# Stick-breaking attention: background passes dealt out otherwise, the logarithm ahead of a copy, VectorE's small work in other places

## The reference, cut to what matters

```
log_keep = where(mask, log_sigmoid(-z), 0)
suffix = reverse_cumsum(log_keep) - log_keep
w = where(mask, exp(log_sigmoid(z) + suffix), 0)
out = w @ v
```

## Time and profile before

| | |
|---|---|
| runs | 2551.66 us median of 3 (2549.52 to 2555.72) |
| profiled execution | 2550.52 us |
| its span, first to last instruction | 2548.7 us |
| mean granted TensorE clock | 0.992 of full speed |
| PE busy | 2456.3 us (96%), 12198 matmuls |
| DVE busy | 1605.5 us (63%) |
| ACT busy | 1094.4 us (43%) |
| POOL busy | 212.7 us (8%) |
| attention stage, first background pass to the product after the stage | 642.4 to 1003.99 us |

### The profile page before, as it was taken

The page is one execution under the profiler, slowest core; times in us unless marked ns, Lnnn a source line. Parts: engine busy times, 40 slices in busy tenths (PEclk is TensorE's granted clock), DMA queues, the critical chain, the costliest instruction groups (busy, mean ns, idle before and its releaser), DMA issues.

```text
span 2548.7 us, 30875 instructions
## 1 busy us (share of the span) xinstructions
PE 2456.3 (96%) x12198; PEld 2011.7 (79%) x12198; DVE 1605.5 (63%) x2065; ACT 1094.4 (43%) x1782; POOL 212.7 (8%) x351
## 2 busy tenths in 40 slices
PE   6999999999999999999999999999999999999997
PEld 5888888888777777878888776887777888888886
DVE  7887565555666666375652555157747767778779
ACT  6665322333666666123421336234435445443333
POOL 0011111111000000100010003000001212200000
PEclk9999999999999999999999999999999999999999
DMA  4223333334122121624123410110232454674432
GB/s 143 91 100 108 100 106 113 105 108 140 63 79 69 52 80 66 251 92 174 40 96 126 132 34 18 50 34 17 76 131 94 156 159 143 212 285 149 149 132 100
DMA packets 139146, 278.50 MB, mean 109 GB/s; under 512 B 16765, under 2 KB 91178, under 8 KB 132218
## 3 DMA queue, kind: packets, MB, share of 16 engines
q1 hardware_dynamic: 109354, 176.52, 20.9%
q0 software_dynamic: 29648, 100.00, 11.1%
HBM read 196.79 MB, written 79.69 MB: 108 GB/s over the span
## 4 chain that ended last, share of the span: by engine, by line
PE 81%; DVE 8%; ACT 5%; DVEq 2%; DMA 2%; issue 2%; ACTq 1%; SPq 0%; POOL 0%
PE ps L2640 32%; PE ps L597 12%; PE ps L3271 8%; PE ps L2891 6%; PE ps L2739 4%; PE ps L2695 2%; PE ps L591 2%; PE ps L2713 2%; PE ps L3165 1%; DVE c L1979 1%; PE ps L2955 1%; PE ps L2876 1%; PE ps L2724 1%; PE ps L3150 1%; PE ps L2804 1%
## 5 line engine op out<-in xcount | busy, mean ns | idle before, releaser
L1894 DVE TENSOR_TENSOR proj_out<-ps,proj_out 128x512 f32<-128x512 f32 x292 | 194.8, 685 | 209.8 <-PE ps L2640 197.1
L2640 PE MATMUL ps<-a_hi,pw_hi 128*128 128x512 f32 x528 | 207.2, 392 | 0.8 <-ACT proj_out L1239 0.8
L2640 PE MATMUL ps<-a_lo,pw_hi 128*128 128x512 f32 x528 | 205.5, 389 | 0.0
L2640 PE MATMUL ps<-t_hi,pw_hi 128*128 128x512 f32 x464 | 182.0, 392 | 0.0
L2640 PE MATMUL ps<-t_lo,pw_hi 128*128 128x512 f32 x464 | 180.7, 389 | 0.0
L2640 PE MATMUL ps<-a_hi,pw_lo 128*128 128x512 f32 x352 | 137.2, 390 | 0.0
L577 DVE TENSOR_TENSOR w_lo<-w_raw,w_hi 128x2048 fp32r<-128x2048 f32 x28 | 64.1, 2288 | 115.8 <-ACT w_hi L573 110.4
L573 ACT ACTIVATE w_hi<-w_raw 128x2048 fp32r<-128x2048 f32 x28 | 53.6, 1913 | 161.9 <-DMA w_raw<-in_w_out 66.0
L1979 DVE TENSOR_TENSOR_SCAN c<-l,r 128x128 f32<-128x128 f32 (+7 forms) x64 | 86.7, 1355 | 54.5 <-ACT l L1363 54.4
L2640 PEld LDWEIGHTS ps<-a_hi,pw_hi 128*128 128x128 f32 x528 | 99.1, 188 | 21.1 <-issue 1.2
L2640 PEld LDWEIGHTS ps<-a_lo,pw_hi 128*128 128x128 f32 x528 | 99.2, 188 | 20.2
(11 more groups left out here) (498 smaller groups left out, 6621.8 us busy)
## 6 DMA issues: line engine op xcount, KB each, us to landing
pw_raw<-in_w_in SPq DMA_DIRECT2D x30, 1024.0 KB, 5.3
hidden_raw<-hidden_forms SPq DMA_DIRECT2D x28, 1024.0 KB, 4.8
projections<-proj_out POOLq DMA_DIRECT2D x88, 256.0 KB, 3.0
w_raw<-in_w_in SPq DMA_DIRECT2D x18, 1024.0 KB, 5.1
pw_raw<-in_w_ff SPq DMA_DIRECT2D x16, 1024.0 KB, 6.3
w_quarter<-in_w_ff SPq DMA_DIRECT2D x16, 1024.0 KB, 7.2
hidden_forms<-proj_out POOLq DMA_DIRECT2D x56, 256.0 KB, 3.2
hidden_forms<-nb POOLq DMA_DIRECT2D x56, 256.0 KB, 3.3
```

Source lines behind the costliest of these rows:

```text
L1894: return dve.tensor_tensor(out_ap(n, j), product_bank(n, o), src, ALU.add)
L2640: last = pe.matmul(product_bank(n, o), w, a[:, k0 + k, t], start=(k == 0 and g == 0), stop=(k == 3 and g == 2))
```

## The change

It deals the same 192 passes of a pair to the steps by a written list, 24, 8, 12, 4, 3, 21, 15, 9, 3, 21, 15, 9, 4, 20, 20, 4, and lets an output end where the running sum is a multiple of 24 (after steps 0, 3, 5, 7, 9, 11, 13, 15). Between scores and turn a step runs no more than three passes (all of them in steps 0 and 15, none where an output has just ended). In pairs 1 to 3, scores(2) now stands ahead of the 24 passes of step 0, and weigh 7 of the pair before stands behind them, right ahead of turn(0). On ScalarE Ln comes ahead of keep_first. On VectorE the attended copies of odd steps go behind clamp(S+2); at step 0 attended copy 6 goes from ahead of the scan to behind it, and end_of_pair behind clamp(2); half_lo goes from steps 4, 5 to 6, 7 and from 12, 13 to 11, 14. The sum of the work of every engine stays as it was.

```diff
--- before.py
+++ after.py
@@ -301,12 +301,9 @@
 
 
         PASSES = 3 * KT
-        FILL_ENDS = (0, 2, 4, 6, 8, 11, 13, 15)
-        fill_upto, fill_after = [], {}
-        for J, end in enumerate(FILL_ENDS):
-            first = len(fill_upto)
-            fill_upto += [PASSES * J + PASSES * (S - first + 1) // (end - first + 1) for S in range(first, end + 1)]
-            fill_after[end] = J
+        FILL_PASSES = (24, 8, 12, 4, 3, 21, 15, 9, 3, 21, 15, 9, 4, 20, 20, 4)
+        fill_upto = [sum(FILL_PASSES[:S + 1]) for S in range(16)]
+        fill_after = {S: upto // PASSES - 1 for S, upto in enumerate(fill_upto) if upto % PASSES == 0}
 
 
 
@@ -1357,10 +1354,10 @@
                     act.wait_ge(m_ready, 16 * i + S + 1)
                     act.activation(L[S % 2][:, 0:w], L[S % 2][:, 0:w], ACT.Exp)
                     act.activation(R[S % 2][:, 0:w], wide(4 + 2 * (S % 2), w), ACT.Relu, bias=-CLAMP)
+                    act.drain()
+                    act.activation(L[S % 2][:, 0:w], L[S % 2][:, 0:w], ACT.Ln, bias=1.0).then_inc(l_ready, 1)
                     if between is not None:
                         keep_first(between)
-                    act.drain()
-                    act.activation(L[S % 2][:, 0:w], L[S % 2][:, 0:w], ACT.Ln, bias=1.0).then_inc(l_ready, 1)
 
                 def keep_first(S):
                     c, qt = step(S)
@@ -1991,24 +1988,27 @@
                 for S in range(16):
                     if S != 1 or i == 0:
                         score_less_sum(S)
-                    if S - 2 in pair_after:
+                    if S % 2 == 0 and S - 2 in pair_after:
                         keep_attended(i, pair_after[S - 2])
                     if S >= 1:
                         keep_second(i, S - 1)
                     elif i:
-                        keep_attended(i - 1, 6)
                         keep_second(i - 1, 15)
-                    if S in (4, 5):
-                        half_lo(n + 1, 1, S - 4)
-                    if S in (12, 13):
-                        half_lo(n + 2, 0, S - 12)
+                    if S in (6, 7):
+                        half_lo(n + 1, 1, S - 6)
+                    if S in (11, 14):
+                        half_lo(n + 2, 0, (11, 14).index(S))
                     if i < 3 or S < 15:
                         suffix_sum(S + 1)
                     if S == 0 and i:
+                        keep_attended(i - 1, 6)
                         score_less_sum(1)
-                        end_of_pair(i - 1)
                     if i < 3 or S < 14:
                         clamp(S + 2)
+                    if S % 2 and S - 2 in pair_after:
+                        keep_attended(i, pair_after[S - 2])
+                    if S == 0 and i:
+                        end_of_pair(i - 1)
                 if i == 3:
                     keep_attended(3, 6)
                     keep_second(3, 15)
@@ -2745,19 +2745,19 @@
                     scores(0)
                     scores(1)
                     pe.wait_ge(*v_kept(NPROJ - 1))
-                else:
-                    weigh(i - 1, 7)
                 for S in range(16):
                     first, upto = fill_upto[S - 1] if S else 0, fill_upto[S]
-                    early = first if S - 1 in fill_after else upto if S == 0 else (first + upto) // 2
-                    if S == 0:
+                    early = first if S - 1 in fill_after else upto if S in (0, 15) else min(first + 3, upto)
+                    if S == 0 and i == 0:
                         filler(first, early)
                     if i < 3 or S < 14:
                         scores(S + 2)
-                    if S:
+                    if S or i:
                         filler(first, early)
-                    elif i == 0:
+                    else:
                         pe.wait_ge(*c_kept(NPROJ - 1, 3))
+                    if S == 0 and i:
+                        weigh(i - 1, 7)
                     turn(S)
                     if S - 1 in pair_after:
                         weigh(i, pair_after[S - 1])
```

## The result

| | before | after |
|---|---|---|
| median of the runs | 2553.95 us (2549.52 to 2555.72, 6 runs) | 2562.75 us (2557.95 to 2567.02, 6 runs) |
| ratio, with its 95% interval | 1 | 1.0036 [1.0025, 1.0046] |
| profiled execution, span | 2550.52, 2548.7 us | 2557.95, 2556.1 us |
| attention stage, first background pass to the product after it | 642.38 to 1003.99: 361.6 us | 642.36 to 1013.06: 370.7 us |
| turn(0) of pair 1 to turn(0) of pair 2 | 90.22 us | 92.59 us |

The change is slower by 0.36 percent, about 9 us (the medians are 8.8 us apart); the stage alone is 9.1 us longer, and the profiled execution as a whole 7.4 us. The work is the same, as one seam-to-seam window of the changed kernel shows against the earlier trace rows (same columns): TensorE's busy time didn't grow, the window did.

A forecast was written before the change was run, and what follows sets the result against it. TensorE was taken to bound the kernel, its stops 5.05 us a pair. Steps +3.6, seams +4.8 and the end +0.75 made +9.2 on 2550.52: 2559.7, said as 2561 for the median; range 2545 to 2569.

The forecast's parts named there:

- The chains of steps 3 and 12: Before turn(4) and turn(13), fewer passes lie beside the chain: new stops of 1.25 and 1.1 us a pair.
- The wait of step 11: half_lo at step 11 waits for ScalarE's w_hi; scan(12) comes 3.1 us later, new stop 1.2 us before scores(14).
- The seam: Between pairs, clamp(3) starts 3.9 us later behind the gating; stops of 3.0 before scores(4) and turn(2) replace 1.33.
- Scores(5) and bank 3: Stop of 0.5 us before scores(5) in place of 0.32; 0.5 at the seam for bank 3's copy, in place of 0.25.
- SP's queue: At the seams, SP's value load and weight block start behind the 24 passes; taken as 0, bounds 0 and 1 us each.
- The end of pair 3: No passes left between weigh(6) and weigh(7) in the last pair: weigh(7) waits 0.75 us.
- What went: The stops at turn(7), turn(11), scores(16) and turn(14) go, 3.15 us a pair, as more passes stand there.
- Ln ahead of the copy: In ScalarE's queue, the chain's sum stays as it was; the next scan can start one copy, 0.6 us, sooner.
- (a): Rival: TensorE's clock falls at the three seams, 5.1 us more, 2566; chance 0.12.
- (b): Rival: no measurable change, half_lo's wait at step 11 costs nothing, 4.8 us less, 2556; chance 0.26.
- (c): Rival: faster, the scan and not ScalarE's queue decides when turn(S+1) gets its Exp, 12 us less, 2539; chance 0.12.

The follow-up runs named there:

- deal by chain: Changed kernel with half_lo and weigh(7) placed as before, and passes dealt by what each step's chain lacks; ratio to the kernel before 0.9960, period 86.20 us.
- even deal with the new seam: Kernel before, its even deal kept, with Ln ahead of the copy, scores(2) ahead of weigh(7) and the 24 passes, gating behind clamp(2); ratio 0.9963, period 87.49 us.
- both undone: Changed kernel with half_lo back at steps 12 and 13 and weigh(7) ahead of the 24 passes, attended copy 6 ahead of scan(1); median 2549.61 us, ratio to before 0.9987.

## Why the prediction was right

The forecast was +9.2 us; the stage is 9.1 us longer, and the ratio makes 9.2 us of the median. The stops are where the forecast put them, and of the sizes that it gave. That the total agrees to the tenth is partly luck. Counted over all pairs, the stops inside them grew by 4.2 us (forecast 3.6) and those at the seams by 3.9 (forecast 4.8), so that the two errors nearly cancel. The profiled execution itself grew by 7.4 us only, since the part behind the stage was 1.7 us shorter; the last section says why.

Point by point:

- **The chains of steps 3 and 12.** Forecast 1.25 and 1.1, measured 1.27 and 1.16. They came with the deal alone and went with the deal by chain, so the cause is shown.
- **The wait of step 11.** Forecast a scan 3.1 us late and a stop of 1.2. Measured: the scan starts 3.0 us later than with half_lo back, VectorE idles 3.71 us ahead of it, and the stop is 1.25. Undoing it took away that stop only in pairs 1 to 3, so the cause is shown.
- **The seam.** Forecast 3.9 us to clamp(3) and stops of 3.0; measured 3.86 and 1.25+1.52 = 2.8. It is the place of weigh(7) and not the gating as such: with weigh(7) ahead of the passes and 12 passes in step 1, as in the even deal with the new seam, the gating still stands behind clamp(2) and no stop is left before scores(4) or turn(2).
- **Scores(5) and bank 3.** Forecast 0.5 and 0.5, measured 0.55 and 0.41. The 0.5 before scores(5) was forecast for pair 0 too, which has no such stop.
- **SP's queue.** I had bounded it by 0 and 1 us a seam and taken 0. In pair 1 ScalarE did wait 0.59 for the weight block (first row), yet its next instruction, Exp(4), started without idle time:

```profile
751.31 1.06 ACT L1347 ACTIVATE w_hi<-w_raw 128x1024 fp32r<-128x1024 f32 x1 [0.59 <-DMA w_raw<-in_w_in]
752.47 0.53 ACT L1355 ACTIVATE l<-l 128x384 f32<-128x384 f32 x1
```

  By VectorE's timeline clamp(4) ended only at 752.43, so the wait cost nothing; but the cover was used up to 0.1 or 0.2 us.
- **The end of pair 3.** Forecast 0.75; weigh(7) idles 0.61 there, 0.77 with the overlap.

```profile
1011.52 0.89 PE L2695 MATMUL ps<-wt,v 128*128 128x256 f32 x4 [0.61 <-DVE out_t L1949]
```

- **What went.** All four old stops and the one before turn(1), as said. But I gave turn(7) 0.83 in each pair from the row of pair 1; in the other three pairs it was 0.55 (idle 0.39 or 0.40). The last pair's turn(14) lost 1.64 and not 0.64, which makes up for most of that. And I credited the deal with all of it, while Ln ahead of the copy takes turn(7) and scores(16) away by itself.
- **Ln ahead of the copy.** I costed it at next to nothing. It is worth 1.4 to 1.75 us in pairs 1 to 3 on the old order. The total came out right all the same, as I read it since the new deal covers most of the same stops, so that the two parts don't add there; no run takes Ln alone back out of the changed kernel. Asked for the parts singly I was wrong, as the expectation for the deal alone shows, with its wrong sign.

The rivals: the clock (a) fell at no seam of the profiled execution. The window from 744 to 752 of the changed kernel, TensorE busy 5.54 of 8 us, has the granted clock at full, and so has the next.

```profile
744.00:752.00 8.00, 5.54 (x28) 3.92 (x27) 6.18 (x9) 4.61 (x7) 0.00 (x0) 1.00 0.65 246
752.00:760.00 8.00, 6.51 (x31) 4.44 (x30) 6.08 (x8) 7.47 (x13) 0.00 (x0) 1.00 0.00 0
```

Split idle time did not add up here as I had read the Trainium skill ("TensorE: Matmul & The Clock Gate", Part 1) to allow; the longest single piece in that stretch was 1.36 us. Nor did it fall at the three seams of the run with half_lo back, which have the same stops. But the length of a stop doesn't settle the clock. In pair 0 a stop of 2.57 us before scores(3) was followed by a fall to 1.2 GHz in seven of the ten traces. The same stop was not in the eighth, shown with the even deal and the new seam, nor were stops of 2.97 (half_lo back) and 2.83 (both undone) in the other two. So these traces show six seams at which the clock held; they don't rule out a fall in another execution. (The stop of the earlier trace rows is the longest of the stage only: in the same trace TensorE stands for 3.27 us at 1439.)

Rival (b) would have needed step 11 to be free, (c) the scan to decide everywhere; the single-edit runs refute the first and leave of the second one step in sixteen.

## What to carry to other kernels

Where one engine is nearly full and others feed it step by step, work out for each step how long the feeding chain is and how much work lies beside it; background work belongs where the chain is longer, not in even shares and not where the step is long anyway. An instruction that waits costs its wait to everything queued behind it on its engine, so see what its producer raises, and when, before it is moved ahead of a scan or a clamp. And measure the edits one by one: here one of four was worth 0.22 percent, and the sum lost 0.36.

## What the runs showed that was not expected

The effects of two edits, read from single periods, added up to 0.01 us. That closeness is luck, as pairs of one trace can differ by 0.3, but a difference such as that of 86.20 and 87.50 is well clear of it, and the timed runs can't tell it.

The part behind the stage, from its end to the end of the span, varied between 1543.0 us (after) and 1553.1 us (weigh(7) ahead), with the same instructions. The granted clock accounts for most of it. I cut that part of each trace into windows of 4 us and added up each window's length times what its granted clock lacks of full speed: 13.1 us for the first and 24.7 us for the second. Less this, they are 1529.9 and 1528.4 us, and all ten traces lie between 1528.4 and 1530.8. The kernel before lost 14.8 us there, 1.7 more than the changed one, and that is why the whole profiled execution grew by 7.4 us where the stage grew by 9.1. Why the clock falls at a place in one execution and not in the next stays open.
